# Side work moved by a few rounds in the two hybrid passes of a long fp32 kernel

## The reference, cut to what matters

```
q, k, logf, v -> hgrn2_chunked                       # levels, lengths 128
cq = l2norm(cq) * GD_DK ** -0.5;  ck = l2norm(ck)    # "lengths": sums of squares
cum = cumsum(g);  decay = exp(cum_t - cum_s)         # "decays"
sol = triangular_solve(eye + lower, rhs)             # the inverse, by doubling
for each chunk of 128 tokens, 4 heads:               # "chain"
    v_new = u - w @ state
    o     = (q * exp(cum)) @ state + scores @ v_new
    state = state * exp(last) + (k * exp(last - cum))^T @ v_new
o_gd = head_rmsnorm(o) * silu(z)
o_rg = rg_lru(conv(rg_x)) * gelu(rg_gate)            # gated linear recurrence ("lru")
return concatenate([o_hg, o_gd, o_rg]) @ w_out       # wo
```

## Time and profile before

| what | value |
|---|---|
| median of 3 runs | 3857.38 us (3857.03 to 3859.34) |
| the profiled execution | 3857.03 us, its span 3855.0 us |
| mean granted TensorE clock | 0.987 |
| PE busy | 3708.9 us, 96% of the span |
| DVE busy | 1886.3 us, 49% |
| ACT busy | 1436.9 us, 37% |
| POOL busy | 170.8 us, 4% |

### The profile page before, as it was taken

The page is one execution under the profiler, slowest core; times in us unless marked ns, Lnnn a source line. Parts: engine busy times, 40 slices in busy tenths (PEclk is TensorE's granted clock), DMA queues, the critical chain, the costliest instruction groups (busy, mean ns, idle before and its releaser), DMA issues.

```text
span 3855.0 us, 46043 instructions
## 1 busy us (share of the span) xinstructions
PE 3708.9 (96%) x18208; PEld 3020.5 (78%) x18208; DVE 1886.3 (49%) x2674; ACT 1436.9 (37%) x2174; POOL 170.8 (4%) x157
## 2 busy tenths in 40 slices
PE   9998899999999998999999999999999999999998
PEld 7776788877668887788877797888888877887887
DVE  4455644456745435433358574333433376563333
ACT  3344333336533332432255443322332264443322
POOL 0003000001100000000000220000000000300000
PEclk9999999999999999999999999999999999999999
DMA  4000222222003222222221012222222221012221
GB/s 175 34 33 33 77 99 99 88 88 96 15 33 112 96 99 88 99 99 98 82 91 57 22 50 89 98 98 86 106 99 99 71 100 47 31 41 99 99 96 62
DMA packets 45285, 306.91 MB, mean 80 GB/s; under 512 B 5136, under 2 KB 5520, under 8 KB 10640
## 3 DMA queue, kind: packets, MB, share of 16 engines
q1 hardware_dynamic: 45072, 303.97, 22.2%
HBM read 301.86 MB, written 2.10 MB: 79 GB/s over the span
## 4 chain that ended last, share of the span: by engine, by line
PE 83%; DVE 10%; ACT 4%; issue 1%; POOL 1%; DMA 0%; DVEq 0%; ACTq 0%; SPq 0%
PE ps L430 81%; DVE split L2030 3%; ACT arena L1141 2%; PE ps L439 2%; DVE arena L2034 2%; DVE X L2034 2%; DVE arena L2030 2%; ACT split L1141 1%; ACT L1141 1%; DVE arena L2850 1%; DVE arena L2026 0%; DVE small L2046 0%; DVE arena L2058 0%; POOL arena L3118 0%; DMA X<-in_x 0%
## 5 line engine op out<-in xcount | busy, mean ns | idle before, releaser
L430 PE MATMUL ps<-split 128*128 128x512 f32 (+2 forms) x13596 | 3103.3, 387 | 80.9 <-DVE X L2034 24.9
L430 PEld LDWEIGHTS ps<-split 128*128 128x128 f32 x13596 | 2487.8, 189 | 618.2 <-issue 67.9
L2030 DVE TENSOR_TENSOR split<-ring,split 128x1024 fp32r<-128x1024 f32 (+1 forms) x554 | 675.2, 1219 | 1273.2 <-ACT split L1141 1257.2
L1141 ACT ACTIVATE split<-ring 128x1024 fp32r<-128x1024 f32 (+1 forms) x554 | 583.0, 1052 | 1353.7 <-PE ps L430 1333.4
L430 PE MATMUL ps<-arena 128*128 128x128 f32 (+9 forms) x3344 | 495.6, 301 | 32.2 <-ACT arena L1141 11.9
L430 PEld LDWEIGHTS ps<-arena 128*128 128x128 f32 (+2 forms) x3344 | 402.6, 193 | 109.9 <-issue 75.6
L1141 ACT ACTIVATE arena<-ps 128x512 f32<-128x512 f32 (+6 forms) x580 | 297.9, 514 | 394.1 <-PE ps L430 222.4
L2030 DVE TENSOR_TENSOR arena<-arena 128x512 f32<-128x512 f32 (+5 forms) x254 | 150.5, 593 | 71.2 <-ACT split L1141 49.8
L1141 ACT ACTIVATE split<-arena 128x512 fp32r<-128x512 f32 x156 | 98.8, 633 | 164.7 <-DVE arena L2030 162.4
L2030 DVE TENSOR_TENSOR arena<-arena,ps 128x512 f32<-128x512 f32 x176 | 121.0, 688 | 40.9 <-PE ps L430 22.0
L2030 DVE TENSOR_TENSOR split<-arena,split 128x512 fp32r<-128x512 f32 x156 | 108.0, 692 | 64.2 <-ACT split L1141 61.6
(11 more groups left out here) (98 smaller groups left out, 980.7 us busy)
## 6 DMA issues: line engine op xcount, KB each, us to landing
ring<-in_wts SPq DMA_DIRECT2D x268, 1024.0 KB, 4.8
ring<-in_wts SPq DMA_DIRECT2D x25, 512.0 KB, 3.4
X<-in_x SPq DMA_DIRECT2D x4, 512.0 KB, 5.6
out<-arena SPq DMA_DIRECT2D x4, 512.0 KB, 2.6
ring<-in_wts SPq DMA_DIRECT2D x2, 784.0 KB, 4.2
C<-in_cb SPq DMA_DIRECT2D x1, 1403.5 KB, 14.1
ring<-in_wts SPq DMA_DIRECT2D x2, 576.0 KB, 10.4
C<-in_cb SPq DMA_DIRECT2D x1, 512.0 KB, 6.2
```

What stands on the lines that cost most here:

```text
L430: return e.matmul(out, l, r, start=start, stop=stop, skip_group_check=True)
L1141: o.sig(a.activation(out, i, f, **kw), sig)
L2030: o.sig(v.tensor_tensor(out, a, b, op), sig)
```

## The change

Five edits, all in `hybrid` (each runs twice):

1. PE, `lengths`: two turns (62 and 64) with four products each, where four turns (62 to 65) had two each.
2. PE, `decays`: two turns (70 and 72) with two each, where 70 to 73 had one each.
3. ACT, `lru`: four idle rounds between the square root and the wait for `lru`, where there were eight.
4. `back` on ACT goes from round t + 7 to t + 6, on DVE from t + 8 to t + 6. PE's `back` stays in round t + 6.
5. DVE's loop over its remaining rounds: a step of `side` behind each of the first four rounds, where there was one behind the first two and two more behind the last round.

```
             for t in range(8):
-                yield from c.to(62 + t // 2)
+                yield from c.to(62 + t // 4 * 2)
                 lengths(t)
...
             for h in range(4):
-                yield from c.to(70 + h)
+                yield from c.to(70 + h // 2 * 2)
                 decays(h)
...
             act(Y.TA, Y.TA, ACT.Sqrt, "lr_a")
-            yield from idle(8)
+            yield from idle(4)
             a.wait_ge(S["lru"], l + 1)
...
-        mix = rounds(16, [None, fresh, None, powers, chunk_root, None, None, back])
+        mix = rounds(16, [None, fresh, None, powers, chunk_root, None, back])
...
-        mix = rounds(16, [None, None, None, state, norm, normed, None, None, back])
+        mix = rounds(16, [None, None, None, state, norm, normed, back])
...
         split(last[0])
         for x, _ in enumerate(mix):
-            if x < 2:
+            if x < 4:
                 next(side)
-        next(side)
-        next(side)
         split(last[1])
```

## The result

| | before | changed |
|---|---|---|
| median | 3857.29 us (4 runs, 3857.03 to 3859.34) | 3889.85 us (4 runs, 3886.12 to 3893.18) |
| profiled execution | 3857.03 us, span 3855.0 | 3885.28 us, span 3883.3 |
| mean granted clock | 0.987 | 0.984 |

The changed kernel is slower by a ratio of 1.0083 (95% interval 1.0065 to 1.0100). The forecast was 3880.4 us, with a range to 3889: direction and waits were right, the clock was sized too small, and the median lies just outside the range. The profiled execution itself is 28.3 us longer, where 23.4 was forecast. First the page: PE's busy time rose by 11.3 us, although the kernel computes the same, and its idle time within the span by 17.0. The forecast's own terms give some 18 us more of idle time and 5 more of busy time, so it is the busy time that it had too low.

The account below looks back on a forecast made before the run. PE was taken as the bound, busy 3708.9 of 3855.0 us. Per pass, -0.9 + 4.4 + 4.0 - 1.3 + 1.9 = +8.1, plus clock 3.6, is 11.7; two passes add 23.4 to 3857.03: 3880.4 us, range 3869 to 3889.

Parts of the forecast that it names:

- clock +3.6: Lower granted clock per pass: 2.6 us behind ACT's long wait, 1.0 in the tail, 0 behind the four 2.0 us waits.
- Lengths: PE's lengths products in two groups instead of four: 0.28 us gained per vanished insertion, two per pass.
- Merging saves ... 0.19 for decays: PE's decays in two groups instead of four: 0.19 us gained at each of two vanished insertions per pass.
- The wait for `inv(21)`: ACT's copies into H[0] hold up its inv(21) copy, so PE waits 4.4 us per pass; bounds 0 and 5.5.
- not slower: Rival: lru comes before ACT finishes inv(20), PE sees no new waits and keeps the gains: 3852.6 us; chance 0.05.
- The bank waits: Chain of chunks: PE waits 2.0 us in rounds 9 and 13 for the bank powers frees; round 14 gains 1.3.
- The tail: Last transposes need normed(15), behind DVE's fourth addition to X: PE waits 1.9 us per pass, plus 1.0 of clock.
- the two additions ... save nothing: DVE's two additions to X, no longer behind the last subtraction, gain 0, since what follows waits for PE.
- The row behind the clock term: Earlier trace: after a 4.49 us PE wait, clock 0.50 for 5.2 us, read as 2.6 us of work lost.
- clock at full speed: Rival: the clock does not fall behind the waits, leaving +2 x 8.1, 3873.2 us; chance 0.12.
- no bank waits: Rival: powers is released sooner, so the chain's 2.0 us waits don't bite: 3872.4 us; chance 0.05.
- every wait drags the clock down: Rival: each 2 us wait also lowers the clock, 4 x 2.6 and 1.6 more per pass in the tail: 3894; chance 0.06.

Follow-up runs that it names:

- e2: Kernel before with back alone moved, to round t+6 on both ACT and DVE: median 3870.52 us, mean +10.8 us, ratio 1.0030.
- e15: Changed kernel with DVE's tail loop as before, two side steps in it and two behind: median 3885.67 us, +24.9 us against the kernel before.
- e7: Kernel before with DVE's back alone moved by one round, to t+7: median 3858.43 us, mean -2.4 us, ratio 0.9996.
- e4: Kernel before with lengths and decays grouped, nothing else: median 3860.29 us, mean -0.8 us, ratio 0.9997.
- e12: Kernel before with all four decays in a row in turn 70: median 3863.67 us, mean +3.8 us, ratio 1.0008.
- e10: Kernel before with ACT's idle(8) in lru as idle(6): median 3867.34 us, mean +6.9 us, ratio 1.0020.
- e9: Kernel before with ACT's idle(8) in lru as idle(5): median 3867.58 us, mean +7.7 us, ratio 1.0020.

## Why the prediction fell short, point by point

The step that failed is the clock: "clock +3.6" per pass, 7.2 in all. The profiled execution lost some 11.4 us to it (an estimate: the rows "clock behind it" of the table, and at the decays what is seen less the gain that was forecast), the mean over ten runs at most 12.4. The forecast had left out the drop at the grouped decays altogether and put those behind the bank waits at nothing.

- **Lengths.** Forecast -0.56 in a pass, seen -0.62. Right.
- **Decays.** "Merging saves ... 0.19 for decays" failed as a mechanism: its bounds, 0 and 1.2 of gain for both edits, had no loss in them. Grouped, the products with four rows are followed by a fall of the granted clock while PE shows no gap, in ten of twelve passes, and single ones in none of 22. Seen are +0.65 and +0.76 us where -0.38 was forecast, so 2.2 us of the 4.3 that the forecast lacks (27.7 - 23.4). The comparison of the changed kernel with single decays gives 4.3 +-3.2, an interval that also takes in the 1.4 us seen at the place itself; whether more is lost elsewhere isn't shown.
- **The wait for `inv(21)`.** Forecast 4.4 with 2.6 of clock; seen 4.71 with 2.92 in the first pass and 1.59 in the second, and +13.6 alone. Right, and the rival "not slower" is ruled out with it: DVE's multiplication ended at 2276.28, 0.03 us before ACT's copies start at 2276.31.
- **The bank waits.** Forecast 2.0 each, 1.3 back in round 14; seen 2.2, 2.2 and 1.4. Right. They stand 34 and 47 us behind the first wait instead of "25 and 37", which were times before without the shift. The clock behind them, taken as 0 with 2.6 as upper end, cost 1.6 behind one of the four in the profile. This was sized too low, and e2's 4 us beyond its waits point the same way.
- **The tail.** Forecast 1.9 + 1.0, seen 2.07 + 1.6 in each pass; by e15 that drop may stand in for one a few microseconds later. But "the two additions ... save nothing" was wrong: DVE has them behind it earlier, and PE's wait at the next norm is 0.6 to 0.8 shorter.
- **The row behind the clock term.** The drop of the earlier trace rows began within the wait: from 1588.0 to 1592.7 us the mean clock was 0.83. Those rows alone, which start behind the wait, don't show what the prediction reads from them on a drop that overlaps a wait.
- **Sum.** The waits and gains were forecast as +16.2 us for both passes; the two passes of the profile have 27.7 - 11.4 = 16.3. Of the rivals, clock at full speed and no bank waits are ruled out by the rows; "every wait drags the clock down" (3894) was nearer than I gave it, but only one of the four bank waits in the profile shows it. That the changed kernel with single decays comes to +23.4, the very forecast, is in part luck: in the rows of the changed kernel more clock behind the waits and a shorter wait at the next norm cancel.
- **The base.** The mean over ten runs of the changed kernel is 3888.0 us, which lies inside the range; the first median lies just outside. Of the 7.6 us to the forecast 3.2 are the base (3857.03 us, where the mean of 95 runs is 3860.3) and 4.3 the change. The first runs of the kernel before lay low in its own spread, and no forecast from one profile could know it.

How the drops fall differs from one profile to the next, so each size here from one profile is a sample; what is settled is the mean over runs, and that the drops come at grouped decays. The cause within the group is open. Whether the four rows of the operand matter, or the length of such products in a row, was not separated, and gaps too short to show beside modelled ends of matmuls are not excluded.

## What to carry to other kernels

A step that waits for another engine, moved ahead in an engine's strict queue, holds everything behind it: find out when the signal really comes, and who waits for what is behind. Where several engines hand banks to each other, follow the loop through all of them, since moving a copy by one round may free a bank in time and by two may close a loop of waits (e7 against e2, which also moves ACT's copy by one). A group of products that use few rows can cost clock where it saves switches, as the decays did here, so its windows' granted clock is to be read even where PE shows no idle time.

## What the runs showed of the hardware

- The granted clock fell to 0.50, its 1.2 GHz level, with PE busy throughout as far as the profile shows: 3.4 us in e4, 6.8 us in e12, at and behind fp32 products with four rows by 512 columns. With two or four such products in a row it fell in ten of twelve passes, with one by one in none of 22. The Trainium skill ("TensorE: Matmul & The Clock Gate", section "HAM oscillation — how this bites in real kernels") puts such drops down to PE idling between bursts; at the decays the traces disagree, behind the 4.54 us wait they agree.
- A wait of 1.9 us was followed by a drop in some places (2325.23 in the changed kernel, 2304.49 in e2) and by none in others (both of e10), and those of 2.8 us (e9) by one in both passes. A short wait's clock cost is thus not a fixed price.
- The same program ran from 3854.2 to 3872.7 us, with a mean clock of 0.987 in the fastest and 0.982 in the slowest run: a lower mean clock goes with a longer time, 2.4 us for each 0.001. A difference of 3 us needed some ten runs of each kernel.
